# Narrow and wide products regrouped over pairs of feed-forward blocks

## What is computed

```
def swiglu(x, w_in, w_down):                  # w_in 1024 x 5632, w_down 2816 x 1024
    gate, up = jnp.split(x @ w_in, 2, axis=-1)
    return (jax.nn.silu(gate) * up) @ w_down

for i in range(DEPTH):                        # DEPTH = 2
    h = h + 0.5 * rmsnorm(swiglu(rmsnorm(h, g1), w_in1, w_down1), g2)
    h = h + rmsnorm(mixer_i(rmsnorm(h, g3)), g4)     # i = 0: gMLP + SSD, i = 1: latent attention
    h = h + 0.5 * rmsnorm(swiglu(rmsnorm(h, g5), w_in2, w_down2), g6)
    gate = jax.nn.sigmoid(rmsnorm(h, g7) @ w_gate)
    h = h + rmsnorm(gate * (p[i] @ w_proj), g8)
```

## Time and profile before

| quantity | value |
|---|---|
| time, median of 3 runs | 1114.08 us (1113.59 to 1114.47) |
| span of the profiled execution | 1112.2 us |
| PE busy | 1101.8 us, 99% of the span |
| PE weight loads busy | 937.5 us, 84% |
| DVE busy | 817.1 us, 73% |
| ACT busy | 570.2 us, 51% |
| mean granted TensorE clock, as a share of full speed | 0.999 |

### The profile page before, as it was taken

The page is one execution under the profiler, slowest core; times in us unless marked ns, Lnnn a source line. Parts: engine busy times, 40 slices in busy tenths (PEclk is TensorE's granted clock), DMA queues, the critical chain, the costliest instruction groups (busy, mean ns, idle before and its releaser), DMA issues.

```text
span 1112.2 us, 14134 instructions
## 1 busy us (share of the span) xinstructions
PE 1101.8 (99%) x5727; PEld 937.5 (84%) x5727; DVE 817.1 (73%) x1074; ACT 570.2 (51%) x706; POOL 82.8 (7%) x138
## 2 busy tenths in 40 slices
PE   9999999999999999999999999999999999999997
PEld 6888888887888888888888888888898888888886
DVE  5876777588997677677786867768876667776775
ACT  7434444567564554444565544445775555444454
POOL 2200000200110200000113000001200020000011
PEclk9999999999999999999999999999999999999999
DMA  8755555645544555555555555555523365555541
GB/s 315 257 189 189 189 190 179 255 171 189 185 176 151 209 217 188 191 189 189 189 200 217 196 190 189 189 189 173 206 78 113 121 243 187 192 188 194 189 172 57
DMA packets 31600, 208.37 MB, mean 187 GB/s; under 512 B 3760, under 2 KB 3808, under 8 KB 8112
## 3 DMA queue, kind: packets, MB, share of 16 engines
q1 hardware_dynamic: 27792, 193.48, 48.6%
q0 software_dynamic: 3600, 13.46, 3.6%
q10 hardware_dynamic: 144, 0.52, 0.1%
HBM read 206.39 MB, written 1.06 MB: 187 GB/s over the span
## 4 chain that ended last, share of the span: by engine, by line
PE 92%; DMA 2%; DVE 2%; issue 2%; ACT 1%; POOL 0%; SPq 0%; DVEq 0%; POOLq 0%
PE PS L721 23%; PE PS L186 17%; PE PS L188 17%; PE PS L187 17%; PE PS L724 12%; DMA raw<-stream 2%; PE PS L383 1%; PE PS L1941 1%; DVE WL L168 1%; ACT WH L161 1%; PE PS L1238 1%; PE PS L1962 1%; PE PS L1943 0%; PE PS L1952 0%; DMA h<-x 0%
## 5 line engine op out<-in xcount | busy, mean ns | idle before, releaser
L168 DVE TENSOR_TENSOR WL<-raw,WH 128x2048 fp32r<-128x2048 f32 x180 | 411.2, 2290 | 154.4 <-ACT WH L161 153.9
L161 ACT ACTIVATE WH<-raw 128x2048 fp32r<-128x2048 f32 x180 | 342.9, 1908 | 116.6 <-DMA raw<-stream 116.5
L721 PE MATMUL PS<-X,WH 128*128 128x512 f32 x1152 | 288.4, 392 | 0.1
L721 PEld LDWEIGHTS PS<-X,WH 128*128 128x128 f32 x1152 | 209.1, 189 | 39.1 <-DVE actb L832 0.3
L724 PEld LDWEIGHTS PS<-X,WL 128*128 128x128 f32 x1152 | 157.2, 190 | 11.3
L724 PE MATMUL PS<-X,WL 128*128 128x256 f32 x1152 | 160.6, 282 | 0.0
L825 ACT ACTIVATE sgb<-sgb 128x256 f32<-128x256 f32 x72 | 30.1, 417 | 226.4 <-DVE sgb L821 226.4
L186 PE MATMUL PS<-WH,X 128*128 128x512 f32 (+3 forms) x360 | 141.0, 392 | 0.8 <-DVE WL L587 0.5
L188 PE MATMUL PS<-WL,X 128*128 128x512 f32 (+3 forms) x360 | 138.7, 385 | 0.0
L187 PE MATMUL PS<-WH,X 128*128 128x512 f32 (+3 forms) x360 | 138.5, 385 | 0.0
L186 PE MATMUL PS<-WH,BH 128*128 128x512 f32 x288 | 113.1, 393 | 0.0
(11 more groups left out here) (280 smaller groups left out, 1316.6 us busy)
## 6 DMA issues: line engine op xcount, KB each, us to landing
raw<-stream SPq DMA_DIRECT2D x181, 1024.0 KB, 4.8
PG<-post_g POOLq DMA_DIRECT2D x8, 512.0 KB, 6.6
QG<-pre_g POOLq DMA_DIRECT2D x7, 512.0 KB, 7.4
Eg<-acs_rows POOLq DMA_DIRECT2D x2, 1024.0 KB, 6.8
raw<-stream SPq DMA_DIRECT2D x3, 512.0 KB, 6.3
h<-x SPq DMA_DIRECT2D x4, 256.0 KB, 4.4
out<-h SPq DMA_DIRECT2D x4, 256.0 KB, 2.0
raw<-stream ACTq DMA_DIRECT2D x1, 512.0 KB, 4.4
```

The lines of the kernel that those rows point to most:

```text
L161: act.activation(WH[:, n % RING, :], raw[:, n % RING, :], ACT.Copy).then_inc(sem("w_hi"), 1)
L168: dve.tensor_tensor(WL[:, n % RING, :], raw[:, n % RING, :], WH[:, n % RING, :], ALU.subtract).then_inc(sem("w_lo"), 1)
L721: pe.matmul(PS[:, bank, :], wh[:, kt, cols], X[:, kt, :, :].rearrange("p a n -> p (a n)"), start=kt == 0, stop=False)
```

## The change

Only `ffn_block_pe` changes. The four passes of a block are now put in an order that depends on the block's number: gate wide, up wide, gate narrow, up narrow for an even block; gate narrow, up narrow, gate wide, up wide for an odd one. The wait for a bank stands ahead of the first pass that writes it, and the semaphore count behind the last. The number of matmuls, their operands and the lists of all other engines are the same. `skip_group_check` is an option of the program builder.

```diff
         def ffn_block_pe(pe, f, v, n):
 
-            gate, up = block_banks(v)
             split_done(pe, n)
             wh = whole(WH, n).rearrange("p (k n) -> p k n", k=KT)
             wl = whole(WL, n).rearrange("p (k n) -> p k n", k=KT)
-            for part, bank in enumerate((gate, up)):
-                if v == 0:
-                    pe.wait_ge(sem("acted" if part else "silu"), 2 * f + 2)
-                else:
-                    last = 0 if v == 1 else v - 2
-                    pe.wait_ge(sem("b_act" if part else "b_scaled"), block_count(f, last))
+            order = ((0, 1), (1, 1), (0, 0), (1, 0)) if v % 2 else ((0, 0), (1, 0), (0, 1), (1, 1))
+            started = set()
+            for i, (part, low) in enumerate(order):
+                bank = block_banks(v)[part]
+                if part not in started:
+                    if v == 0:
+                        pe.wait_ge(sem("acted" if part else "silu"), 2 * f + 2)
+                    else:
+                        last = 0 if v == 1 else v - 2
+                        pe.wait_ge(sem("b_act" if part else "b_scaled"), block_count(f, last))
                 cols = slice(part * P, (part + 1) * P)
                 for kt in range(KT):
-                    pe.matmul(PS[:, bank, :], wh[:, kt, cols], X[:, kt, :, :].rearrange("p a n -> p (a n)"),
-                              start=kt == 0, stop=False)
-                for kt in range(KT):
-                    ins = pe.matmul(PS[:, bank, 0:SEQ], wl[:, kt, cols], XH[:, kt, :], start=False, stop=kt == KT - 1)
-                ins.then_inc(sem("w_used" if part else "b_gate"), 1)
+                    opens, closes = kt == 0 and part not in started, kt == KT - 1 and part in started
+                    if low:
+                        ins = pe.matmul(PS[:, bank, 0:SEQ], wl[:, kt, cols], XH[:, kt, :], start=opens, stop=closes,
+                                        skip_group_check=True)
+                    else:
+                        ins = pe.matmul(PS[:, bank, :], wh[:, kt, cols], X[:, kt, :, :].rearrange("p a n -> p (a n)"),
+                                        start=opens, stop=closes, skip_group_check=True)
+                if part in started:
+                    ins.then_inc(sem("w_used" if part else "b_gate"), 1)
+                started.add(part)
```

## The result

The changed kernel takes **1122.5 us** (median of 4 runs, 1121.2 to 1123.4) against 1113.9 us before: the ratio is 1.0075, 95% interval 1.0064 to 1.0087. The forecast was 1120.0 us with a range of 1117.6 to 1122.6. The direction and the main cause came out as forecast; the loss is 8.6 us where the sum had 5.9. The median lies 0.1 us inside the upper end of the range, and two of the four runs lie above it.

A forecast was written before the change was run, and what follows sets the result against it. PE was taken as one stream bounding the kernel. Waits in blocks 0 and 1 +7.5, spacing -2.1, `acted` +0.1 and last pairs +0.4 gave +5.9 on 1114.1: 1120.0 us, range 1117.6 to 1122.6.

The forecast's parts named there:

- The wait in block 1: Before block 1's up, PE waits for block 0's `actb`: 1.9 us in three stages, +1.7 in f = 2.
- the entries that go in blocks 0 and 1: Blocks 0 and 1 lose two narrow-to-wide entries per stage, saving 0.04 us each stage, 0.2 us in all.
- the 0.1 for `acted` in f = 2: Block 0's up reaches its wait for `acted` 0.95 us earlier, costing 0.1 us once, in f = 2 only.
- +1.7: Blocks 0 and 1 of f = 2: `actb` ends when it did, but PE has 4.60 us left behind it, not 2.89.
- The spacing: Fewer changes between narrow and wide matmuls, about 0.02 us saved each, 0.06 per pair: -2.1 us, bounds 0 and -4.2.
- The Trainium skill's rule: Full-array weight loads would not overlap matmuls, so regrouping would gain 0 and the sum be 2.1 us higher.
- The last pair: Second block's `b_lo` comes 0.5 us later against 0.5 slack before the down product: 0.1 us per stage, +0.4 in all.
- The clock: Rival: PE's wait before block 1's up lowers its clock, adding 7 us over four waits: 1127 us; chance 0.05.
- a rate of half behind the wait: Sign of being wrong: PE's matmuls behind block 1's wait for `actb` run at half rate.
- The argument against it: The longest wait in the body before, 1.0 us, left the mean granted clock at 0.999.
- a worse tail: Rival: block 17's `b_lo` passes on its whole delay, +0.65 us a stage instead of 0.1: 1122.2 us; chance 0.07.
- The Trainium skill's warning: The clock drops to half in longer gaps between bursts of matmuls; cited for PE's wait before block 1's up.

The follow-up runs named there:

- mult_first: The changed kernel, but DVE does block 0's `usum` and `actb` before it splits unit u+6; 1112.98 us, ratio 0.9988 to the kernel before.
- pairs_only: The changed kernel with the old order of passes in blocks 0 and 1; 1113.03 us, ratio 0.9988 to the kernel before.
- nested: The changed kernel with gate wide, gate narrow, up narrow, up wide in every block; 1112.35 us, ratio 0.9988 to the kernel before.
- long_wait: The changed kernel, but DVE splits units u+6 and u+7 between block 0's scale and its `usum`, to lengthen PE's wait to 4.2 us; 1137.94 us.
- filled twin: The changed kernel with PE's block 1 wait lengthened to 4.2 us and 18 extra wide matmuls, results thrown away, ahead of it; 1130.10 us.
- fill: The changed kernel with 8 extra wide matmuls, results thrown away, ahead of block 1's wait for `actb` in each feed-forward stage; 1120.72 us.
- first_two_only: The kernel before with the changed order in blocks 0 and 1 only; 1122.13 us, ratio 1.0074 to the kernel before.

## Why the prediction was right, and where its sum was off

**The wait in block 1** was forecast at 1.9 us, with its place, releaser and cause. The trace has 1.88, 1.87, 2.03 and 1.88 from the starts, and mult_first shows the cause. With the entries that go in blocks 0 and 1 and the 0.1 for `acted` in f = 2, the sum had 7.4 for these stretches; without the fall of the clock they measure 7.9. What the sum left out is the 0.1 behind the wait, in each stage. It could have been read before: in f = 2 of the kernel before, the wide pass behind the wait for `actb` took 1.94 us where 1.84 is usual, and the forecast used that 1.94 for the kernel before but an ordinary 0.95 for the changed one. In f = 2 I had +1.7 because `actb` was set by the arrival of unit u+6, and it came to +2.0: 0.1 is the one just named, and 0.2 came because the unit itself arrived that much later after the stage's start, ACT's part ending at 616.52. The 0.1 for `acted` there cost nothing, since PE waited for `actb` in any case.

**The spacing** was right in the term and in size: 0.42 us for seven pairs, as 7 x 0.06 had it; 3.83 us for a narrow run of 32 where 3.82 stood. The Trainium skill's rule ("TensorE: Matmul & The Clock Gate", "What overlaps and what doesn't") would have made this 0, and pairs_only and nested show -1.25 and -1.46. The rule does not describe this kernel's full-array loads: in the changed kernel too they are busy for 938.2 us beside matmuls busy for 1102.8 in a span of 1121.3.

**The last pair** is a term that was mis-sized: 0.1 us of waiting per stage was put, and the trace adds 0.21 behind BL. DVE in the last pair of f = 1, as the earlier trace rows, PE's weight load that waits, and PE around it:

```profile
539.05 0.69 DVE L820 TENSOR_REDUCE gsum<-PS 128x256 f32<-128x512 f32 x1 [0.96 <-PE PS L726]
...
546.10 0.68 DVE L820 TENSOR_REDUCE usum<-PS 128x256 f32<-128x512 f32 x1
...
547.73 0.42 DVE L848 TENSOR_TENSOR BL<-actb,BH 128x256 fp32r<-128x256 f32 x1 [0.48 <-ACT BH L844]
```
```profile
548.21 0.19 PEld L186 LDWEIGHTS PS<-WH,BH 128*128 128x128 f32 x1 [0.36 <-DVE BL L848]
```
```profile
547.88 0.39 PE L188 MATMUL PS<-WL,BH 128*128 128x512 f32 x1
548.21 0.50 PE L186 MATMUL PS<-WH,BH 128*128 128x512 f32 x1
548.55 0.40 PE L187 MATMUL PS<-WH,BL 128*128 128x512 f32 x1
```

The chain ran as described, and DVE's idle time before `usum` is used up. PE's matmul comes 548.21 - 547.88 = 0.33 after the one ahead of it instead of 0.227, 0.10 late. What the sum left out is the restart: the next matmul follows after 0.34 us instead of 0.227. The load of the matmul that waited starts together with it, at 548.21, where loads otherwise start about 0.22 ahead; that this is what delays the next one is likely but not shown. So a wait of PE cost its length and 0.1 on top, here and in block 1.

**The clock** is the step that failed in its weight. It stood among the rivals at 0.05, at 7 us for falls behind all four waits, and a rate of half behind the wait was named as a sign of being wrong; f = 0 shows that sign. The runs show the rival in part: a fall behind one of the four waits in the profiled run, at 1.5 us, and clocks that fit the same in two more of the four. The argument against it was that the longest wait before, 1.0 us, had left the clock alone; that says nothing of 1.9 us, and I should have taken part of the price into the forecast. That the time stayed in the range is partly luck: its upper part was meant for a worse tail, and the fall of the clock filled it. long_wait and its filled twin show that the standstill is the cause for 4.2 us; for 1.9 us the same cause is likely, with fill's five runs at 0.998 and above for it. The Trainium skill's warning ("TensorE: Matmul & The Clock Gate", "Why this matters for your kernels") held, at a shorter gap than the page puts: the two falls traced behind short waits came with PE idle for 1.7 us (changed kernel, f = 0) and 1.8 us (first_two_only, f = 2).

**What stays open**: 0.70 us of the 9.1 between the profiled executions lie in the opening (+0.50) and the other stages. At the same place the other kernels' traces stand between -0.7 and +0.2 (opening) against the same trace of before. So the opening varies by nearly a microsecond between kernels that are alike up to there; the changed kernel's +0.50 lies outside those values, with PE's waits for the load of h and for a split longer by 0.3 and 0.4 in sum. I take this as the spread between executions, but no run separates it from an effect.

With all terms as measured in the profiled run, 7.9 - 1.8 + 0.7 + 1.5 = +8.3, beside 8.6 between the medians.

## What to carry to other kernels

Before PE's passes are put in another order, look at what stands in the lists of the engines between the moved end and the moved wait: here a 2.3 us split on DVE that had been hidden turned a gain of 1.3 us into a loss of 8.6, and moving one line of DVE's list gave it back. Treat a wait of PE as dearer than its length: 0.1 us for the restart, and the danger of a slower clock (seen behind one wait of 1.9 us in four, behind every one of 4.2); if the wait can't go, matmuls without use ahead of it were cheaper than standing still, by 7.8 us over four waits of 4.2. Where no wait can be afforded, an order that only mirrors neighbours (wide, narrow, narrow, wide) got two thirds of the grouping's gain per pair without moving any deadline.

## What the runs showed of the hardware that was not expected

- Behind PE's waits of 1.7 to 1.9 us the granted clock fell once in each of two traces and at varying places (f = 0 in one, f = 2 in the other), behind waits of 4.1 to 4.2 us all four times in one trace. The latter cost 1.2 to 2.7 us a time, 2.0 on average; with matmuls filled into the same wait the clock stayed up in every run (0.998).
- A change from 256 to 512 moving columns and back costs 0.020 us in groups of 8, about 0.017 in groups of 4 and 0.0065 when they alternate.
- Behind a wait of PE the second matmul follows late by 0.1 us: after 0.34 us instead of 0.227 when they are wide, and eight narrow ones take 1.06 instead of 0.95.
